# Expert stage of a hybrid SSD / HGRN2 / mixture-of-experts layer: each pass's token rows picked by one-hot products on TensorE in place of gathering DMAs

## The reference

```python
def hier_moe(h, w_gr, b_gr, w_er, b_er, w_gate, w_up, w_down):
    ...
    p_grp, grp = lax.top_k(g_prob, 1)
    ...
    top_v, top_i = lax.top_k(e_logits, MOE_TOP_K)
    weight = p_grp * jax.nn.softmax(top_v, axis=-1)
    expert = grp * MOE_EXPERTS_PER_GROUP + top_i
    ...
    def expert_block(args):
        xr, e = args
        return (jax.nn.silu(xr @ w_gate[e]) * (xr @ w_up[e])) @ w_down[e]
```

## Time and profile before

| what | value |
|---|---|
| median of 3 runs | 1836.8 us (1835.54 to 1837.95) |
| the profiled execution: time, span of its trace | 1840.5 us, 1838.7 us |
| PE busy | 1722.8 us, 94% of the span |
| PE weight loads (PEld) | 1056.8 us, 57% |
| DVE busy | 897.6 us, 49% |
| ACT busy | 487.8 us, 27% |
| POOL busy | 480.1 us, 26% |
| moved by DMA | 344.35 MB, mean 187 GB/s |
| mean granted TensorE clock | 0.979 of full |

### The profile page before, as it was taken

One profiled execution on the slowest core, in us unless ns is written; L12 is line 12 of the kernel. 1 busy time (PEld: TensorE's weight loads), 2 busy tenths in 40 slices (PEclk: granted clock), 3 DMA queues, 4 the chain that ended last, 5 costly groups with the idle time before them and its releaser, 6 DMA issues.

```text
span 1838.7 us, 19778 instructions
## 1 busy us (share of the span) xinstructions
PE 1722.8 (94%) x7344; PEld 1056.8 (57%) x7344; DVE 897.6 (49%) x1428; ACT 487.8 (27%) x839; POOL 480.1 (26%) x516
## 2 busy tenths in 40 slices
PE   5999999999999999999999999999898887988877
PEld 2555555555647888888886488885533332333332
DVE  3626545456358879787786786663420000000004
ACT  3221422413324454444443100003221101111112
POOL 1214142141447656756555000000010000010000
PEclk9999999999999999999999999999899999999999
DMA  7221323322321121121222444567779999999996
GB/s 306 96 80 57 115 69 92 110 73 69 104 69 35 35 58 46 34 57 34 57 84 88 155 132 129 168 215 280 277 314 430 428 430 429 429 372 430 430 425 248
DMA packets 153985, 344.35 MB, mean 187 GB/s; under 512 B 15462, under 2 KB 105791, under 8 KB 140858
## 3 DMA queue, kind: packets, MB, share of 16 engines
q1 hardware_dynamic: 136048, 319.45, 46.0%
q10 hardware_dynamic: 13114, 15.89, 2.6%
q0 software_dynamic: 4752, 8.05, 1.2%
HBM read 333.54 MB, written 19.09 MB: 192 GB/s over the span
## 4 chain that ended last, share of the span: by engine, by line
PE 69%; DVE 13%; DMA 8%; issue 7%; ACT 2%; POOL 1%; SPq 1%; DVEq 0%; POOLq 0%; ACTq 0%
PE bank L945 12%; PE bank L2066 10%; PE bank L2946 9%; PE bank L986 6%; PE bank L2964 6%; PE bank L586 4%; DMA arena<-in_w_up_dram 3%; PE bank L2108 3%; DVE arena L1747 2%; PE bank L536 2%; DMA arena<-in_w_down_dram 2%; PE bank L1030 2%; PE bank L1574 1%; PE bank L1592 1%; PE bank L1038 1%
## 5 line engine op out<-in xcount | busy, mean ns | idle before, releaser
L945 PE MATMUL bank<-stay,arena 128*128 128x512 f32 (+1 forms) x704 | 240.0, 496 | 0.0
L2946 PE MATMUL bank<-arena 128*64 128x512 f32 x832 | 186.3, 604 | 16.9 <-DMA arena<-in_w_up_dram 8.3
L945 PEld LDWEIGHTS bank<-stay,arena 128*128 128x128 f32 x704 | 132.5, 190 | 99.7 <-issue 92.3
L2946 PEld LDWEIGHTS bank<-arena 128*64 128x64 f32 x832 | 66.1, 139 | 132.5 <-issue 117.9
L2964 PE MATMUL bank<-arena 128*64 128x512 f32 x416 | 108.5, 681 | 33.8 <-issue 15.8
L1464 POOL TENSOR_TENSOR arena<-arena 128x256 f32<-128x256 f32 x112 | 89.0, 794 | 172.7 <-DVE arena L1728 125.9
L3096 DVE TENSOR_TENSOR arena<-arena,bank 128x512 f32<-128x512 f32 x17 | 11.7, 687 | 233.4 <-PE bank L2946 233.4
L986 PE MATMUL bank<-arena,stay 128*128 128x512 f32 x256 | 114.6, 595 | 3.1 <-DVE arena L1239 3.1
L2816 POOL DMA_INDIRECT y_dram<-arena x16 | 16.1, 1007 | 384.4 <-DVE arena L3103 383.8
L3102 DVE COPY arena<-bank 128x512 f32<-128x512 f32 x16 | 11.1, 691 | 190.5 <-PE bank L2964 190.5
L2066 PE MATMUL bank<-stay,arena 128*128 128x256 f32 x456 | 103.1, 379 | 0.0
(11 more groups left out here) (492 smaller groups left out, 3007.6 us busy)
## 6 DMA issues: line engine op xcount, KB each, us to landing
arena<-in_w_gate_dram SPq DMA_DIRECT2D x24, 2048.0 KB, 18.4
arena<-in_w_down_dram SPq DMA_DIRECT2D x24, 2048.0 KB, 22.4
arena<-in_w_up_dram SPq DMA_DIRECT2D x22, 2048.0 KB, 22.3
arena<-in_w_in_dram SPq DMA_DIRECT2D x58, 512.0 KB, 4.0
arena<-in_w_ada_dram SPq DMA_DIRECT2D x12, 2048.0 KB, 10.7
stay<-in_w_gate_dram SPq DMA_DIRECT2D x8, 2048.0 KB, 21.2
stay<-in_w_up_dram SPq DMA_DIRECT2D x8, 2048.0 KB, 17.9
arena<-in_w_in_dram ACTq DMA_DIRECT2D x6, 2048.0 KB, 9.7
```

The lines of the kernel that those rows point to most:

```text
L945: mm = pe.matmul(ps[:, 0:n], w[:, k, :], hT[:, k, o:o + n], start=(k == 0), stop=(k == KT - 1))
L2946: mm = pe.matmul(b[cols, :], xgT[r][:, k, cols], w[u][:, k, :], start=(k == 0), stop=(k == KT - 1))
```

## The change

The rows of every pass are no longer gathered from DRAM but made on chip, as those of the first pass were: DVE makes a one-hot matrix for the pass (`choose`: eight 128x128 operations that compare the slot numbers with each token's place and multiply by the reciprocal root mean square, and one 128x512 addition), PE multiplies it with the resident `xl` (`gather`: eight products 128x128 by 128x512 into banks 0 and 1), DVE copies the result to `xg` (`gathered`), and PE transposes it as before (`turn_rows`). `h2`, its four stores, the 17 gathering DMAs and their index column go. There is now one `xg`. The rows of the final pass and of the first loop pass are made in the last step ahead of the loop (and the second pass of step 8 in step 7): there a second `gather` stands between the halves of `down`. ACT does `gated_columns` ahead of `columns`. In `route_tensor` 12 products into bank 7, whose results nobody reads, stand ahead of the first real one. SP no longer waits for the stores ahead of chunk 3.

```diff
-            def normalised(cc):
-                act.wait_ge(s_xl2, cc + 1)
-                act.activation(h2[:, cc, :], xl[:, cc, :], ACT.Identity, scale=rst[:, 4 + cc:5 + cc]).then_inc(s_h2, 1)
-
             def whole(cc):
                 residual_squares(cc, 0)
                 residual_squares(cc, 1)
                 residual_rstd(cc)
-                normalised(cc)
...
-        xg = [take(D) for _ in range(2)]
+        xg = take(D)
+        row_hots = [take(LCH, P) for _ in range(2)]
...
+            for i in range(2 * LCH):
+                pe.matmul(bank[7][:, (i % 4) * P:(i % 4 + 1) * P], ident[:, :], xl[:, i // 2, 0:P], start=True, stop=True)
+            for i in range(LCH):
+                pe.matmul(bank[7][:, :], ident[:, :], xl[:, i, 0:512], start=True, stop=True)
...
-            for cc in range(LCH - 1):
-                store_rows(cc)
             sp.wait_ge(s_mo, 2 * LCH)
             load(0, 2, static_pair(0))
-            store_rows(LCH - 1)
-            sp.wait_ge(s_h2st, 16 * LCH)
+            sp.wait_ge(s_xl, 2 * LCH)
             sp.wait_ge(s_iota, INDEX_ROWS)
             load(1, 0, static_pair(1))
...
-            gather(1, gidx[:, COLUMN[1]:COLUMN[1] + 1])
             for p in range(PASSES):
-                if p + 2 <= PASSES + 1:
-                    pool.wait_ge(s_xgt, p + 1)
-                    gather(p % 2, gidx[:, COLUMN[p + 2]:COLUMN[p + 2] + 1])
                 pool.wait_ge(s_yb, p + 1)
                 scatter(p % 2, sidx[:, COLUMN[p]:COLUMN[p] + 1])
...
+                if p >= 1:
+                    act.wait_ge(s_d, p)
+                gated_columns(p)
                 if p + 1 < PASSES:
                     if p >= 1:
                         act.wait_ge(s_u, p)
                     columns(p + 1, (p + 1) % 2)
-                if p >= 1:
-                    act.wait_ge(s_d, p)
-                gated_columns(p)
+                if step == TWICE - 1:
+                    act.wait_ge(s_u, p + 1)
+                    columns(p + 2, p % 2)
+            act.wait_ge(s_u, PASSES)
+            columns(PASSES, 0)
+            columns(PASSES + 1, 1)
             act.wait_ge(s_rv, LISTS)
...
+            def gather(q):
+                pe.wait_ge(s_oh, q)
+                pe.wait_ge(s_xgc, q)
+                for hf in range(2):
+                    for cc in range(LCH):
+                        mm = pe.matmul(bank[hf][:, :], row_hots[0][:, cc, :], xl[:, cc, hf * 512:(hf + 1) * 512],
+                                       start=(cc == 0), stop=(cc == LCH - 1))
+                    mm.then_inc(s_gp, 1)
+
+            def turn_rows(q):
+                pe.wait_ge(s_xe, q)
+                x = xg.rearrange("p (c k) -> p k c", k=KT)
                 for k in range(KT):
                     mm = pe.transpose(bank[k // 4][:, (k % 4) * P:(k % 4 + 1) * P], x[:, k, :], ident[:, :])
                 mm.then_inc(s_xgt, 1)
...
+                    gather(q + 1)
                     pe.wait_ge(s_guc, p)
                     turn_gated(r, p)
+                    turn_rows(q + 1)
                     pe.wait_ge(s_yb, p)
                     down(c + 2, landed(c + 2), p)
...
-                if p + 1 < PASSES:
-                    rows(1 - r, arrived(p + 1), p + 1)
+                gather(p + 1)
                 if p:
                     pe.wait_ge(s_guc, p)
                 turn_gated(r, p)
+                turn_rows(p + 1)
                 if p:
                     pe.wait_ge(s_yb, p)
-                down(c + 2, landed(c + 2), p)
+                if step == TWICE - 1 or p + 1 == PASSES:
+                    def second_set():
+                        gather(p + 2)
+
+                    down(c + 2, landed(c + 2), p, second_set)
+                    turn_rows(p + 2)
+                else:
+                    down(c + 2, landed(c + 2), p)
...
-                rows(1, OVER_GATHERS + 16 + i * 16, PASSES + i)
-                pe.wait_ge(s_xgc, PASSES + 1 + i)
+                pe.wait_ge(s_xgc, PASSES + 2 + i)
                 pe.wait_ge(s_sig, PASSES + i)
                 up(OVER, 1, landed(OVER) + i * 32, bank[2], s_g)
                 pe.wait_ge(s_gu, PASSES + i)
                 up(OVER + 1, 1, landed(OVER + 1) + i * 32, bank[3], s_u)
+                gather(LOOP_ROWS + 1 + i)
                 pe.wait_ge(s_guc, PASSES + i)
                 turn_gated(1, PASSES + i)
+                turn_rows(LOOP_ROWS + 1 + i)
...
+            def choose(q, column=None):
+                if column is None:
+                    dve.tensor_scalar(slot_now, slot_now, float(-2 * SLOT), None, ALU.add).then_inc(s_cs, 1)
+                else:
+                    dve.tensor_scalar(slot_now, slot8, float(-2 * SLOT * column), None, ALU.add).then_inc(s_cs, 1)
+                dve.wait_ge(s_cs, q * STEPS_OF_SET - 2 * LCH)
+                for k in range(2):
+                    for cc in range(LCH):
+                        j = k * LCH + cc
+                        dve.scalar_tensor_tensor(row_hots[k][:, cc, :], iof, slot_now[:, j:j + 1],
+                                                 rst[:, 4 + cc:5 + cc].broadcast_to([P, P]), ALU.is_equal, ALU.mult).then_inc(s_cs, 1)
+                dve.wait_ge(s_cs, q * STEPS_OF_SET)
+                dve.tensor_tensor(row_hots[0], row_hots[0], row_hots[1], ALU.add).then_inc(s_oh, 1)
+
+            def gathered(q):
+                dve.wait_ge(s_gp, q * 2 - 1)
+                dve.wait_ge(s_xgt, q)
+                dve.tensor_copy(xg[:, 0:512], bank[0][:, :])
+                dve.wait_ge(s_gp, q * 2)
+                dve.tensor_copy(xg[:, 512:1024], bank[1][:, :]).then_inc(s_xe, 1)
+
+            choose(1, COLUMN[1])
             dve.wait_ge(s_cleared, YD_CLEARED)
             for step in STEP:
                 p = FIRST_PASS[step]
                 of_step = [p, p + 1] if step == TWICE else [p]
                 for q in of_step:
                     gated(q % 2, q, bank[3] if q == p else bank[2])
+                last = of_step[-1]
+                gathered(last + 1)
+                choose(last + 2, COLUMN[last + 2] if last + 2 <= LOOP_ROWS else None)
+                if step == TWICE - 1 or last + 1 == PASSES:
+                    gathered(last + 2)
+                    choose(last + 3, COLUMN[last + 3] if last + 3 <= LOOP_ROWS else None)
```

More of the change, by code:

```diff
@@ L2372, in build @@
         yb = [take(D) for _ in range(2)]
-        gidx = take(NB).bitcast(U32)
+        slot8 = take(NT)
+        slot_now = take(NT)
         sidx = take(NB).bitcast(U32)
@@ L2424, in build @@
         s_w = [sem(f"expert_weights_loaded{r}") for r in range(4)]
-        s_xg = [sem(f"rows_gathered{r}") for r in range(2)]
+        s_oh = sem("row_choices_ready")
+        s_gp = sem("rows_gathered")
         s_xgt = sem("rows_transposed_for_experts")
@@ L2489, in route_scalar @@
             act.wait_ge(s_rp, FIRST_HALF)
-            act.copy(xg[0][:, 0:512], bank[0][:, :])
+            act.copy(xg[:, 0:512], bank[0][:, :])
             act.wait_ge(s_rp, FIRST_GATHERED)
-            act.copy(xg[0][:, 512:1024], bank[1][:, :]).then_inc(s_ra, 1)
+            act.copy(xg[:, 512:1024], bank[1][:, :]).then_inc(s_ra, 1)
         def route_tensor(pe):
@@ L2865, in experts_scalar @@
                 if step == TWICE:
-                    act.wait_ge(s_u, p)
-                    columns(p + 1, (p + 1) % 2)
                     act.wait_ge(s_gut, p - 1)
@@ L2892, in experts_scalar @@
             with act.Fori(0, n) as i:
-                act.wait_ge(s_u, PASSES + i)
-                columns(PASSES + i, 1)
                 act.wait_ge(s_gut, PASSES + i)
@@ L2898, in experts_scalar @@
                 gated_columns(PASSES + i)
-            act.wait_ge(s_u, PASSES + n)
-            columns(PASSES + n, 0)
+                act.wait_ge(s_u, PASSES + i + 1)
+                columns(PASSES + 2 + i, 1)
             act.wait_ge(s_ct, CHOICES_TURNED)
@@ L2922, in experts_tensor @@
         def experts_tensor(pe):
-            def rows(r, loaded, done):
-                pe.wait_ge(s_xg[r], loaded)
-                if done is not None:
-                    pe.wait_ge(s_xgc, done)
-                x = xg[r].rearrange("p (c k) -> p k c", k=KT)
+            def gather(q):
[8 more added lines that the diff above has]
+                pe.wait_ge(s_xe, q)
+                x = xg.rearrange("p (c k) -> p k c", k=KT)
                 for k in range(KT):
@@ L2954, in turn_gated, with down @@
                 mm.then_inc(s_gut, 1)
-            def down(chunk, loaded, done):
+            def down(chunk, loaded, done, between=None):
                 w = weights_of(chunk)
@@ L2965, in down @@
                                            start=(f == 0), stop=(f == FT - 1))
+                    if hf == 0 and between is not None:
+                        between()
                 mm.then_inc(s_d, 1)
-            def arrived(p):
-                return 16 * (p // 2 + p % 2)
             for step in STEP:
@@ L2976, in experts_tensor @@
                     q = p + 1
```

(3 more changed lines are left out.)

41 lines of the change are left out of this document (11 added, 30 removed).

## The result

The changed kernel takes 1874.5 us (median of 4 runs, 1871.97 to 1875.89) against 1836.2 us before (median of 4, 1835.32 to 1837.95): a ratio of 1.0204, with a 95% interval of 1.0192 to 1.0217. It is 2.0% slower, 38 us. The forecast was 1871 us with a range of 1858 to 1885.

The account below looks back on a forecast made before the run. The weight stream bounds the kernel before, and PE becomes the bound after. Pass 0's start at 1339.4, plus 487.4 for the stage and 46.3 for the end, gives a 1873.1 us span, hence 1871 us; range 1858 to 1885.

Parts of the forecast that it names:

- full-width price: PE's sets of eight products: 16 records in 7.03 us, 6.87 us back to back; 17 sets make 117 us.
- half-width row: Gate and up's half-width products, 32 records in 7.07 us, would price a set at 3.5 us; taken as lower bound.
- The order's gain: Up to down in a step: 8.9 us instead of 4.65, then down 7.09 us instead of 8.78.
- 87 us of slack: PE from pass 0 to the loop pass's down: 60.5 us of waits and 27 us of lost clock.
- Do the weights keep up: Ordinary steps: weights and scatter need 29.3 to 30.5 us beside PE's 29.7; a smaller lead would add 6 us.
- the loop pass: After step 13: gate waits 3.07 us for ACT's eight operations, then 29.7 us, together 32.8 us.
- pass 0's start: Start of the stage, taken as 1339.4 us; earlier stores and ACT work for h2 priced at nothing.
- The 12 unread products: In routing, filling a 5.23 us wait: taken as 0, with -2 and +4 us in the range.
- the end: Last down to span's end: a chain of DMAs, 46.3 us instead of 52.4.
- the gathers' 9.4 us: Indirect queue in the stage: gathers move 4.0 MB, worth 9.4 us of the weight stream at 429 GB/s.
- the first rival: Weights stay the bound through the stage and 9.4 us of bytes go: 1827 us; 3 in 100.
- From the profiled execution to the median: Whole kernel: span plus 1.8 us for the execution, less 3.7 us to the median, 1873.1 to 1871 us.

Follow-up runs that it names:

- ACT's old order: The changed kernel with ACT's eight row operations ahead of its copy of the gated tile again, in all ordinary steps: 1941.5 us, one run.
- without gathers in the new order: Kernel before without its 17 gathers (stale rows), with gated transposes ahead of row transposes and ACT's copy ahead of its eight operations: 1821.4 us, ratio 0.9916.
- four sets where PE waited for weights: Kernel before with the change's PE and ACT orders, rows of passes 2, 4, 6 and 12 picked by products, others gathered: 1830.4 us, ratio 0.9967.
- three in and near step 8 and ahead of the loop: Kernel before with the change's PE and ACT orders, rows of passes 8, 10 and the final one picked by products, others gathered: 1843.5 us, ratio 1.0032.
- the new order alone: Kernel before, gathers kept, with gated transposes ahead of row transposes and ACT's copy ahead of its eight operations: 1835.4 us, ratio 0.9988.

## Why the prediction was right

The side, the mechanism and the size held: PE became the bound, at the full-width price. By its own steps, in the profiled execution (the chain's 7.08 us of a set have the last product's drain in them, which the 6.87 leave out):

| term | predicted | measured |
|---|---|---|
| a set of eight products | 6.87 us | 7.08 us on the chain |
| ordinary step | 29.7 us | 29.75 us |
| step 7, step 8 | 37.7, 52.3 us | 38.0, 52.2 us |
| step 13 and the wait for ACT | 37.7 + 3.1 us | 41.3 us |
| loop pass, gate to down | 29.7 us | 32.9 us |
| pass 0 starts | 1339.4 us | 1336.9 us |
| pass 0 to the last down | 487.4 us | 491.9 us |
| from there to the span's end | 46.3 us | 45.2 us |
| span | 1873.1 us | 1874.1 us |

- **The price of a set.** The choice between the full-width row (7.03 us) and the half-width row (3.5 us) decided the forecast, and the full-width row was right. The kernel with four products, which leaves out half of the residual rows, shows what the other price would have given: a set of 3.65 us, and 1830 us.
- **The order's gain** was right: a set hides DVE's gated product and the row transposes hide ACT's copy. Both halves, 3 us of wait and 1.7 of clock, show in the run with ACT's old order, where they cost 67 us; that is about 5 us for each step that has the wait. 17 sets of 7.08 us are 120 us, and the stage grew by 45 us (446.9 to 491.9): 75 of the 87 us of slack were used, and only because the order gave the waits back.
- **Do the weights keep up:** yes. PE waits for no weights in the stage, nor in the final pass.
- **Mis-sized: the loop pass.** "the last transposes end step 13, so gate waits for ACT's eight operations, 3.07 us as now; then 29.7 us" had the wait but not the clock. Gate behind it took 10.04 us for 32 records, the window shows 0.50 of the clock for its first 3.1 us, and the pass took 3.2 us more:

```profile
1795.94 10.04 PE L2933 MATMUL bank<-arena 128*64 128x512 f32 x32 [3.26 <-ACT arena L2825]
```

  The row of before, 7.09 us behind 3.07, was the cheap case: over the 14 traces the same gate behind 3.06 to 3.26 us took 7.09 us three times, 8.4 to 8.8 us six times and 9.8 to 10.04 us five times. This is most of the 4.5 us that the stage is longer than forecast; the rest is 0.3 us in step 7, 0.5 in step 13 and its wait, and 0.6 over eleven ordinary steps.
- **Mis-sized: pass 0's start.** It came 2.5 us earlier, and the change is not shown to be why. The mixer's last full-width product ended 0.9 us earlier, which varies from kernel to kernel here (1306.4 to 1310.2 us); from there to pass 0 it is 28.1 us instead of 29.8. Of the 14 traces nine have 28.1 to 28.2 us and five 29.0 to 29.8. Among the nine are kernels made from the one before, with its stores and ACT's work for `h2` (28.2 us without gathers in the new order); among the five is the changed kernel with sets of four.
- **The 12 unread products** were priced rightly at nothing, and the way was foreseen. The first set took 7.13 us on PE's timeline in the five traces that have them, and 7.53 to 9.06 us in the nine that don't. But behind them the first product after the choices starts 1.6 us later (15.1 instead of 13.5 us after the mixer's last full-width product, with and without them in the changed kernel), which takes the gain back.
- **Right in size, wrong in kind: the end.** The prediction kept a chain of DMAs there and shortened it to 46.3 us. The timeline of after shows another chain:

```profile
1831.49 1.01 POOL L2804 DMA_INDIRECT y_dram<-arena  x1 [0.51 <-issue]
...
1834.57 2.12 SPq L2790 DMA_DIRECT2D arena<-y_dram  x4
...
1836.79 1.88 SPq L2691 DMA_DIRECT2D stay<-in_w_down_dram  x4
...
1845.68 3.65 PE L3046 MATMUL bank<-stay,arena 128*64 128x512 f32 x16 [0.73 <-ACT arena L2837]
...
1852.89 3.65 PE L3046 MATMUL bank<-stay,arena 128*64 128x512 f32 x16
```

  SP reloads 5.7 us after down's end (1828.86), not 9.7 as before: from the last scatter to the reload it is 3.1 us (1834.57 - 1831.49) instead of 7.1, on a queue with room. The last down (L3046) waits only for ACT's copy, its second half for nothing: the weights are there. So the end is bound by PE's gate, up, down and sums and by ACT's and DVE's closing work, and the near agreement (45.2 against 46.3 us) is luck.
- **Mis-sized: the gathers' 9.4 us** are 12.0 us. It changed no number here, as PE was the bound, but it would have given the first rival 1825 instead of 1827 us. A sum in that rival is off as well: 487.4 - 17 x (6.9 - 4.0) is 438.1 and not 437.5 us, which moves nothing.
- **From the profiled execution to the median.** Before, the profiled execution was 3.7 us above the median; after, 1.4 us. These 2.3 us, with 1.0 us in the span, are the whole miss of 3 us. That the span came out within 1.0 us is luck in part: 4.5 us too little for the stage stand against 2.5 us too late a start and 1.1 us too long an end.

Against the rule of the Trainium skill (Perfetto Trace Analysis, section Identifying Performance Opportunities) that a kernel generally gets faster by improving its most-contended engine, the runs of this case stand so: the engine that carried most, the DMA engines, was relieved of 12 us, and the time rose by 38 us. Where the relief came without the products, 12.0 us did come back. So the rule isn't refuted; what it leaves out is what the relief costs the next engine.

Left open: how much of the gathers' price the bare packets are, and what decides how much clock PE loses behind a wait, at the first set and at the loop pass.

## What to carry to other kernels

Before moving work from a busy resource to one that stands behind it, sum the second one's slack over the stage, waits and lost clock both (here 87 us), and price the new work by a row of its own shape; then ask stage by stage whether the first really bounds there. A relief is worth having only in those places: four sets where PE waited for weights made the kernel 0.3% faster, three in and near step 8 and ahead of the loop made it 0.3% slower, and the trace puts most of that on the one in step 8, where PE was the bound. An order of instructions that is worth next to nothing under one bound (1.5 us here, at the edge of what the measurement tells) can be worth 67 us under the other (ACT's half of it alone), so measure it together with the change that it serves.

## What the runs showed of the hardware

- Indirect gathers whose indices are all out of bounds still issue all packets (4752 in the queue, as before). The medians put their cost at about 3 us of a full stream for all 17, with intervals that overlap.
- A wait of some 3 us didn't cost the same each time, in traces of kernels whose PE work around it is nearly the same. The loop pass's gate took 7.09 us behind 3.07 us, 8.78 us behind 3.07 us in the new order alone, and 10.04 us behind 3.26 us in the changed kernel. The clock ahead of the wait doesn't decide it: in the changed kernel it was 1.00 up to the wait and 0.50 behind it, and in the kernel with ACT's old order it was 1.00 before, in and behind a wait of 3.17 us, and gate took 7.09 us. What does decide it was not found. Behind 3.58 us (ACT's old order) down took 8.4 to 9.95 us in the ordinary steps, and never 7.
- Gate and up of one pass took 13.73 to 13.76 us on the chain in all steps shown here into which PE came without a wait, at a clock of 1.00, so a difference from that number is a quick reading of lost clock.
